# Output gate formed ahead of the norm factor, weight pieces alone on SP's DMA queue, seven expert blocks issued by ScalarE, and another rounding order at the delta products

## The chip, the cores and the metric

The kernel runs on 1 core of one Trainium2 chip, in float32. The metric is the device time of one execution in microseconds. A run of a kernel is given with its span (first to last instruction) and the granted clock of TensorE (PE). The other engines are VectorE (DVE), ScalarE (ACT), GpSimd (POOL) and SyncE (SP), which here only issues DMAs.

## What is computed

Two transformer layers over 256 tokens of width 1024; the second adds 16 meta tokens. The part around the change is the end of the second layer's mixer and its mixture of experts:

```python
o = rms_norm_2(o, out_norm_g) * jax.nn.silu(zf)               # o: sum of the forward and the backward delta rule
y_d = o.reshape(bsz, seq_len, V_WIDTH) @ w_delta
merged = jax.nn.sigmoid(gate_f) * y_f + jax.nn.sigmoid(gate_d) * y_d
h = h + merged @ w_out
hn = rms_norm_2(h, norm_g)                                    # then a router: top group of 8, top 2 of its 8 experts
out = sum over chosen experts e of weight * (silu(hn @ w_gate[e]) * (hn @ w_up[e])) @ w_down[e]
```

There are 64 experts of width 256; gate and up together are 2 MB an expert, down 1 MB: 201 MB that all have to be read.

## The kernel before

**Engines and order.** Every engine has its own program written out by hand, with counting semaphores between them. `fill(name, ...)` gives a PSUM bank to a result, `full[b]` and `free[b]` count its fills and releases, `got(name)` waits for a fill. DMAs start in the order of the issuing engine's program, and an engine that waits holds back everything behind it, its DMA issues too. In this kernel SP issues all loads; ScalarE issues only two of the four stores at the end.

**Products with float32 accuracy from rounded parts.** A weight is cut into a high part (ScalarE, `ACT.Copy` to fp32r) and a low part (POOL, raw minus high), an activation likewise (ScalarE high, DVE low). `matmul3` then makes three products: high x low, high x high, low x high. `w_delta` and `w_out` come as 16 pieces (`N_PARTS`) of 512 KB, eight each, in five buffers (`PART_SETS`); piece n+5 may be loaded when piece n has been used (`part_done`, `load_part`). A piece is 24 products of 128x128 by 256 columns. ScalarE cuts it in `round_part(n)` (L1819), POOL in L2975. The first two pieces of each weight are taken together in `first_two` (L889): it goes through the activation in four pairs of rows and waits for each pair's high part (`h_hi`), then for its low part.

**The norm and the gate of o.** DVE adds up o in `add_out` (L2583) and counts `o_b`. ScalarE squares it (`out_squares`, L1829, into `o_sq`), PE sums the squares (`norms`, fill `no`), ScalarE takes the root (`norm_sqrt`, L1657), DVE the reciprocal and its split (`factors`, L2361 to L2366), and PE spreads the factor over the partitions (`out_spread`, L1220, fills `os00` to `os11`). `out_gated(j)` on DVE (L2699) multiplies a pair of heads in PSUM by o and the gain `out_g` (L2702), and then by silu(z), which lies in `z_g` (L2704). `delta_hi(j)` (L1841) rounds the result, `out_lo(j)` (L2706) makes the low part, and PE starts on `wd0`, the first two pieces. The results `wd0` to `wd3` are gated with `g_g` and added to the Fourier part (L2725, L2726), rounded by `sum_hi(j)` (L1847), and go on to `wp0` to `wp4`, the output product. Then follow the router and the lists of chosen tokens.

**Experts.** 16 groups of 4 experts. A group needs four `gate_up` blocks and two `down` blocks of 2048 KB. Groups 0, 2, ... use `gate_up[0]`, four slots of the weight ring; groups 1, 3, ... `gate_up[1]`. `down` has three buffers, `down_a`, `down_b`, `down_c`. A block of a later group is loaded into a buffer when the group there has been used (`part_used`, `gate_up`, `down`). The eleven blocks that have room at first are issued before group 0 starts. Block j of `gate_up[0]` lies in ring slot (2, 3, 0, 1)[j]; slot 2 held `qd`, slot 3 `z_g` and `g_g`, and slots 0 and 1 hold weight pieces, so blocks 3 and 2 wait for the last two pieces (`part_done(14)`, `part_done(15)`).

**SP's order in this stretch** (L3076 to L3111): pieces 0 and 1; after `o_b` 4 the router's weights and block 0 of group 0; after the last product on block `GD + 1` pieces 2 to 4, two down blocks, pieces 5 to 12, block 2 of group 1, pieces 13 to 15, block 3 of group 1; after the last merged rows block 1 of groups 0 and 1; then blocks 3 and 2 of group 0 and 0 of group 1.

Of the kernel before, what the change touches and what calls it, by code (L numbers as in the profile page):

```python
# [70 lines left out]
def build(nc, A):  # L71
    f32, f32r = mybir.dt.float32, mybir.dt.float32r
    ALU, ACT, AX = mybir.AluOpType, mybir.ActivationFunctionType, mybir.AxisListType
    ctx = ExitStack()
    with ctx:
        sems = {}

        def sem(name):
            if name not in sems:
                sems[name] = ctx.enter_context(nc.semaphore(name))  # L80
            return sems[name]
# [47 lines left out]
        def col(name, j=0):  # L129
            a = COLS[name][0]  # L130
            return cols[:, a + j:a + j + 1]
# [10 lines left out]
        full = [sem(f"bank{b}_full") for b in range(8)]  # L142
        free = [sem(f"bank{b}_free") for b in range(8)]
        fills, uses, turn, readers = {}, [0] * 8, {}, {}
# [16 lines left out]
        WHOLE_SLOT = (0, 1, 0, 1, 2, 3, 0, 1)  # L161
# [15 lines left out]
        N_PARTS, PART_SETS = 16, (0, 1, 4, 2, 3)  # L177
# [66 lines left out]
        o_T, y_delta_lo_r = chunked(both(HEADS * SEQ), HEADS)  # L244
# [166 lines left out]
        down_a, down_b = (place(BLOCK) for _ in range(2))  # L411
# [50 lines left out]
        def two(bank):  # L462
            return bank[:, :].rearrange("p (j t) -> p j t", j=2)
# [972 lines left out]
        def _(act):  # L1436
# [68 lines left out]
            f = got("c")  # L1505
# [146 lines left out]
            def norm_sqrt(name, n, ready, signal, lead=True):  # L1652
                f = fills[name]
                if lead:
                    lead_for(name)
                act.wait_ge(sem(ready[0]), ready[1])
                link(nc.scalar.activation(f.bank[:, 0:n], f.bank[:, 0:n], ACT.Sqrt))  # L1657
                act.sem_inc(sem(signal), 1)
# [56 lines left out]
            def take_gate(kind, j):  # L1715
                f = got(f"{kind}{j}")
                gate, func = {"zz": (z_g, ACT.Silu), "gd": (g_g, ACT.Sigmoid)}[kind]
                link(nc.scalar.activation(gate[:, j], two(f.bank), func))
                act.sem_inc(free[f.b], 1)
                act.sem_inc(sem("z_g"), 1)  # L1720
# [98 lines left out]
            def round_part(n):  # L1819

                arrived, count = part_in(n)
                act.wait_ge(arrived, count)
                nc.scalar.activation(set_hi[part_set(n)], set_raw[part_set(n)], ACT.Copy).then_inc(sem("w_hi"), 1)
# [5 lines left out]
            def out_squares(half):  # L1829
                act.wait_ge(sem("o_b"), 2 * half + 2)  # L1830
                heads = slice(4 * half, 4 * half + 4)
                link(nc.scalar.activation(o_sq[:, heads, :], o_T[:, heads, :], ACT.Square))
                act.sem_inc(sem("o_sq"), 1)

            out_squares(0)
            out_squares(1)
            norm_sqrt("no", SEQ, ("ss_o", 1), "sd_o")
            take_gate("gd", 3)
            round_part(2)

            def delta_hi(j):  # L1841

                act.wait_ge(sem("h_rows"), 8 + j + 1)
                nc.scalar.activation(y_delta_hi_r[:, 2 * j:2 * j + 2, :], two(fills[f"os{j // 2}{j % 2}"].bank),
                                     ACT.Copy).then_inc(sem("h_hi"), 1)

            def sum_hi(j):  # L1847

                act.wait_ge(sem("h_rows"), 12 + j + 1)
                nc.scalar.activation(y_sum_hi_r[:, 2 * j:2 * j + 2, :], two(fills[f"wd{j}"].bank), ACT.Copy).then_inc(sem("h_hi"), 1)  # L1850

            for j in range(4): delta_hi(j)
            round_part(3)
            round_part(4)
            for j in range(4):
                sum_hi(j)
                round_part(2 * j + 5)
                round_part(2 * j + 6)
            round_part(13)
# [97 lines left out]
        def _(dve):  # L1957
            def got(name):
                f = fills[name]
                dve.wait_ge(full[f.b], f.n + 1)  # L1960
                return f
# [3 lines left out]
            def link(ins):  # L1965

                chain[0] += 1
                ins.then_inc(sem("dve_chain"), 1)
                dve.wait_ge(sem("dve_chain"), chain[0])
# [613 lines left out]
            def add_out(l):  # L2583
                f = got(f"o{l.key}")
                o = o_T[:, l.hs[0]:l.hs[0] + 4, l.at - META:l.at - META + P]
                link(nc.vector.tensor_tensor(o, o, four_of(f.bank), ALU.add))
                dve.sem_inc(free[f.b], 1)
                dve.sem_inc(sem("o_b"), 1)
# [106 lines left out]
            for l in (b0, b1, f0, f1): take_values(l)  # L2695
            dve.wait_ge(sem("o_first"), 4)
            for l in (f0, b0, f1, b1): add_out(l)

            def out_gated(j):  # L2699
                f = got(f"os{j // 2}{j % 2}")  # L2700
                o = two(f.bank)
                link(nc.vector.scalar_tensor_tensor(o, o_T[:, 2 * j:2 * j + 2, :], col("out_g"), o, ALU.mult, ALU.mult))  # L2702
                dve.wait_ge(sem("z_g"), j + 1)
                nc.vector.tensor_tensor(o, o, z_g[:, j], ALU.mult).then_inc(sem("h_rows"), 1)  # L2704

            def out_lo(j):  # L2706
# [280 lines left out]
        def _(sp):  # L2987
# [28 lines left out]
            def load_gate_up(q, u, js=range(PER)):  # L3016
                for j in js:
                    name = "odd_in" if u else f"slot{WHOLE_SLOT[4 + j]}_in"
                    sp.dma_start(gate_up[u][j], of_group("gate_up", q, j)).then_inc(sem(name), 16)
                    sp.sem_inc(sem("late_odd" if u else "late_even"), 16 if u else 32)  # L3020
# [14 lines left out]
            def load_down_first(q, u):  # L3035

                sp.dma_start(down[u][0], of_group("down", q, 0)).then_inc(sem("down_c_in" if u else "down_a_in"), 16)

            def load_down_second(q):

                sp.dma_start(down_b, of_group("down", q, 1)).then_inc(sem("down_b_in"), 16)
                sp.sem_inc(sem("late_down"), 16)
# [27 lines left out]
            def load_part(n):  # L3070

                if n >= 5:
                    part_done(n - 5)
                sp.dma_start(set_raw[part_set(n)], FRONT[WD + n // 4][:, n % 4 * QUARTER:(n % 4 + 1) * QUARTER]).then_inc(part_in(n)[0], 16)
# [4 lines left out]
            load_part(1)  # L3079
            sp.wait_ge(sem("o_b"), 4)  # L3080
            sp.dma_start(w_router, A["w_router"]).then_inc(sem("router_in"), 16)
            load_gate_up(0, 0, [0])
            last = readers[f"block{GD + 1}"]
            sp.wait_ge(full[last.b], last.n + 1)
            load_part(2)
            load_part(3)
            load_part(4)
            load_down_first(0, 0)
            load_down_second(0)
            for n in range(5, 13): load_part(n)  # L3090
            load_gate_up(1, 1, [2])
            for n in range(13, N_PARTS): load_part(n)
            load_gate_up(1, 1, [3])
            sp.wait_ge(sem("merged2"), 4)
            load_gate_up(0, 0, [1])
            load_gate_up(1, 1, [1])
            part_done(14)
            load_gate_up(0, 0, [3])
            part_done(15)
# [150 lines left out]
```

## Time and profile before

| | |
|---|---|
| median of 3 runs | 1168.56 us (1168.13 to 1171.38) |
| the profiled execution | 1165.79 us, span 1164.0 us, mean clock 0.938 |
| busy | PE 1015.5 us (87%), PEld 799.3, DVE 508.6, ACT 380.5, POOL 427.6 |
| matmuls | 8121 |
| read from HBM | 302.67 MB |
| chain that ended last | PE 51%, DMA 26%, DVE 14% |

The profiled execution is one run. Its times are microseconds from the start of the span. "SPq" and "ACTq" are the sequencers' own instructions, DMA issues among them; a bracket at the end of a timeline row gives the idle time before it and what ended that. In the chain each piece is work that the end waited for. The clock is given as a share of the full 2.4 GHz. Matmuls overlap, so the duration of a single one is longer than its step in the chain.

### The profile page before, as it was taken

To read this page: it belongs to the slowest core of one execution; us is meant where nothing else is said; L and a number is where in the kernel's file an instruction comes from. 1 tells how busy PE (TensorE), PEld (TensorE's weight loads), DVE (VectorE), ACT (ScalarE), POOL (GpSimd) and SP (SyncE) were. 2 spreads that over 40 slices of the span, in tenths; PEclk is the share of its full clock that TensorE was granted. 3 is DMA by queue.
4 is the path that set the end of the run, shared out by engine and by line. 5 is a ranking of instruction groups with operands and counts; after the bars stand their busy time and mean duration, and the time that the engine had idled before them with its cause. 6 is when DMAs were issued, how large, how long until landed. Compare 5 with 4: busy or idle time off the path is not lost.

```text
span 1164.0 us, 20100 instructions
## 1 busy us (share of the span) xinstructions
PE 1015.5 (87%) x8121; PEld 799.3 (69%) x8121; DVE 508.6 (44%) x979; ACT 380.5 (33%) x572; POOL 427.6 (37%) x192
## 2 busy tenths in 40 slices
PE   9999999999999998899989899977667676676687
PEld 7999999999999998798989798433223232333232
DVE  4356965601136887768864634222222222222213
ACT  5554353444447556335343344100000000000002
POOL 5767868888876856333031271000000000000000
PEclk8999999999999999999999899988888888888889
DMA  7645546566656545115211789999999999999995
GB/s 247 212 134 151 178 128 183 179 183 186 188 172 212 150 124 162 56 54 218 81 66 37 311 284 409 379 426 428 427 428 427 428 428 428 429 427 429 426 424 230
DMA packets 43569, 304.75 MB, mean 262 GB/s; under 512 B 5092, under 2 KB 5476, under 8 KB 30952
## 3 DMA queue, kind: packets, MB, share of 16 engines
q1 hardware_dynamic: 43208, 303.21, 69.2%
q8 instruction: 51, 0.84, 0.3%
q10 hardware_dynamic: 288, 0.52, 0.1%
q14 instruction: 22, 0.18, 0.1%
HBM read 302.67 MB, written 1.05 MB: 261 GB/s over the span
## 4 chain that ended last, share of the span: by engine, by line
PE 51%; DMA 26%; DVE 14%; issue 3%; POOL 2%; ACT 2%; SPq 2%; DVEq 0%; ACTq 0%; POOLq 0%
DMA arena<-gate_up 24%; PE bank L486 10%; PE bank L487 9%; PE bank L488 9%; PE bank L1363 7%; PE bank L871 3%; PE bank L1384 3%; DVE arena L2352 2%; POOL rounded L2975 1%; DMA weights<-front 1%; DVE arena L2099 1%; POOL rounded L2934 1%; DVE arena L2551 1%; DVE arena L2549 1%; DMA arena<-down 1%
## 5 line engine op out<-in xcount | busy, mean ns | idle before, releaser
L2934 POOL TENSOR_TENSOR rounded<-weights,rounded 128x1024 fp32r<-128x1024 f32 x152 | 370.4, 2464 | 160.3 <-ACT rounded L1449 150.5
L486 PE MATMUL bank<-rounded 128*128 128x256 f32 (+2 forms) x776 | 219.7, 283 | 2.3 <-POOL rounded L2934 2.3
L487 PE MATMUL bank<-rounded 128*128 128x256 f32 (+2 forms) x776 | 217.1, 280 | 0.0
L488 PE MATMUL bank<-rounded 128*128 128x256 f32 (+2 forms) x776 | 216.7, 279 | 0.0
L1449 ACT ACTIVATE rounded<-weights 128x1024 fp32r<-128x1024 f32 x146 | 147.4, 1052 | 81.0 <-PE bank L488 49.4
L486 PE MATMUL bank<-rounded,rounded 128*128 128x256 f32 (+3 forms) x552 | 159.1, 288 | 3.7 <-DVEq L2354 1.6
L487 PE MATMUL bank<-rounded,rounded 128*128 128x256 f32 (+3 forms) x552 | 156.7, 284 | 0.0
L488 PE MATMUL bank<-rounded,rounded 128*128 128x256 f32 (+3 forms) x552 | 156.5, 284 | 0.0
L486 PEld LDWEIGHTS bank<-rounded 128*128 128x128 f32 (+1 forms) x776 | 145.7, 188 | 4.4 <-POOL rounded L2934 3.0
L487 PEld LDWEIGHTS bank<-rounded 128*128 128x128 f32 (+1 forms) x776 | 145.7, 188 | 0.7 <-issue 0.7
L488 PEld LDWEIGHTS bank<-rounded 128*128 128x128 f32 (+1 forms) x776 | 145.4, 187 | 0.0
L1363 PE MATMUL bank<-arena 128*32 128x512 f32 x512 | 73.6, 738 | 50.7 <-DMA arena<-gate_up 50.7
L1363 PE MATMUL bank<-weights,arena 128*32 128x512 f32 x512 | 69.3, 702 | 49.2 <-DMA weights<-gate_up 48.1
L486 PEld LDWEIGHTS bank<-rounded,rounded 128*128 128x128 f32 (+1 forms) x552 | 103.8, 188 | 6.7 <-issue 1.9
L487 PEld LDWEIGHTS bank<-rounded,rounded 128*128 128x128 f32 (+1 forms) x552 | 103.8, 188 | 0.2
L488 PEld LDWEIGHTS bank<-rounded,rounded 128*128 128x128 f32 (+1 forms) x552 | 103.7, 188 | 0.1
L2842 DVE TENSOR_TENSOR arena<-arena,bank 128x256 f32<-128x256 f32 x16 | 6.8, 422 | 211.6 <-ACT arena L1908 211.6
L1363 PEld LDWEIGHTS bank<-arena 128*32 128x32 f32 x512 | 17.8, 131 | 100.9 <-DMA arena<-gate_up 52.4
L1363 PEld LDWEIGHTS bank<-weights,arena 128*32 128x32 f32 x512 | 17.8, 127 | 95.2 <-issue 95.2
L1908 ACT ACTIVATE arena<-bank 128x256 f32<-128x256 f32 x16 | 6.1, 384 | 230.4 <-PE bank L1363 230.4
L1396 PE MATMUL bank<-arena 128*128 128x512 f32 x128 | 59.3, 605 | 12.6 <-DVE arena L2847 12.6
L1327 PEld LDWEIGHTS bank<-arena 128*128 128x128 f32 x512 | 59.5, 192 | 8.3 <-issue 8.3
(467 smaller groups left out, 1445.1 us busy)
## 6 DMA issues: line engine op xcount, KB each, us to landing
weights<-front SPq DMA_DIRECT2D x165, 512.0 KB, 4.2
arena<-down SPq DMA_DIRECT2D x31, 2048.0 KB, 21.6
weights<-gate_up SPq DMA_DIRECT2D x28, 2048.0 KB, 34.3
arena<-gate_up SPq DMA_DIRECT2D x28, 2048.0 KB, 33.3
weights<-front SPq DMA_DIRECT2D x4, 2048.0 KB, 8.1
weights<-gate_up SPq DMA_DIRECT2D x8, 768.0 KB, 13.2
arena<-gate_up SPq DMA_DIRECT2D x4, 1536.0 KB, 33.3
weights<-gate_up SPq DMA_DIRECT2D x4, 512.0 KB, 6.2
```

The costliest lines, as they stand in the source:

```text
L486: nc.tensor.matmul(out, a[0], b[1], start=start, stop=False)
L487: nc.tensor.matmul(out, a[0], b[0], start=False, stop=False)
L488: return nc.tensor.matmul(out, a[1], b[0], start=False, stop=stop)
L871: last = nc.tensor.matmul(f.bank[:, j * n:(j + 1) * n], w[:, c:c + P], x[:, k, :], start=k == 0, stop=k == KD - 1)
L1327: last = nc.tensor.matmul(o, m_tok[:, t, k * P:(k + 1) * P], pick_m[:, t, :], start=t == 0, stop=t == TT - 1)
L1363: last = nc.tensor.matmul(banks[3][j * CAP:(j + 1) * CAP, :], xg[:, k, j * CAP:(j + 1) * CAP], gate_up[u][j][:, k * 2 * FE:(k + 1) * 2 * F ...
L1384: last = nc.tensor.matmul(banks[5 + half][j * CAP:(j + 1) * CAP, :], hid_T[:, i, j * CAP:(j + 1) * CAP], down[u][j // 2][:, c:c + 512], st ...
L1396: nc.tensor.matmul(banks[b][:, :], pick_T[:, i % 2 * P:(i % 2 + 1) * P], yb[:, i // 2 * 512:(i // 2 + 1) * 512], start=True, stop=True).th ...
L1449: nc.scalar.activation(w_hi[h % SPLIT][:, quarter(q)], raw[q % RAW], ACT.Copy).then_inc(sem("w_hi"), 1)
L2099: link(nc.vector.scalar_tensor_tensor(s, r[:, h, :], wi[:, t * NH + h:t * NH + h + 1], causal if h == 0 else s, ALU.mult, ALU.add))
L2352: link(nc.vector.scalar_tensor_tensor(dst[:, lo:hi], x[:, first + lo + s:first + hi + s], tap(j), dst[:, lo:hi], ALU.mult, ALU.add))
L2934: nc.gpsimd.tensor_tensor(lo, raw[q % RAW], hi.bitcast(f32), ALU.subtract).then_inc(sem("w_lo"), 1)
```

## The change

Four edits. DVE multiplies `z_g` in place by o and `out_g`, four heads at a time, right after `add_out`; `out_gated` then only multiplies the spread factor by it. On ScalarE `round_part(2)` moves from ahead of the four `delta_hi` to behind them. SP no longer loads seven expert blocks: ScalarE issues block 0 of group 0 and the first down block behind `out_squares(1)`, the second down block and blocks 2 and 3 of group 1 behind `norm_sqrt`, and block 1 of groups 0 and 1 behind `sum_hi(3)`. On SP piece 2 is loaded once the sum of squares (`no`) is there, pieces 3 to 15 from the end of block `GD + 1` on, with nothing between them, and the wait for the merged rows is gone.

```diff
--- before.py
+++ after.py
@@ -1832,11 +1832,26 @@
                 link(nc.scalar.activation(o_sq[:, heads, :], o_T[:, heads, :], ACT.Square))
                 act.sem_inc(sem("o_sq"), 1)
 
+            def load_even(j):
+
+                act.dma_start(gate_up[0][j], A["gate_up"][0, j]).then_inc(sem(f"slot{WHOLE_SLOT[4 + j]}_in"), 16)
+                act.sem_inc(sem("late_even"), 32)
+
+            def load_odd(j):
+
+                act.dma_start(gate_up[1][j], A["gate_up"][1, j]).then_inc(sem("odd_in"), 16)
+                act.sem_inc(sem("late_odd"), 16)
+
             out_squares(0)
             out_squares(1)
+            load_even(0)
+            act.dma_start(down_a, A["down"][0, 0]).then_inc(sem("down_a_in"), 16)
             norm_sqrt("no", SEQ, ("ss_o", 1), "sd_o")
+            act.dma_start(down_b, A["down"][0, 1]).then_inc(sem("down_b_in"), 16)
+            act.sem_inc(sem("late_down"), 16)
+            load_odd(2)
+            load_odd(3)
             take_gate("gd", 3)
-            round_part(2)
 
             def delta_hi(j):
 
@@ -1850,10 +1865,14 @@
                 nc.scalar.activation(y_sum_hi_r[:, 2 * j:2 * j + 2, :], two(fills[f"wd{j}"].bank), ACT.Copy).then_inc(sem("h_hi"), 1)
 
             for j in range(4): delta_hi(j)
+            round_part(2)
             round_part(3)
             round_part(4)
             for j in range(4):
                 sum_hi(j)
+                if j == 3:
+                    load_even(1)
+                    load_odd(1)
                 round_part(2 * j + 5)
                 round_part(2 * j + 6)
             round_part(13)
@@ -2695,12 +2714,13 @@
             for l in (b0, b1, f0, f1): take_values(l)
             dve.wait_ge(sem("o_first"), 4)
             for l in (f0, b0, f1, b1): add_out(l)
+            dve.wait_ge(sem("z_g"), 4)
+            for half in range(2):
+                z = z_g[:, 2 * half:2 * half + 2].rearrange("p j k t -> p (j k) t")
+                link(nc.vector.scalar_tensor_tensor(z, o_T[:, 4 * half:4 * half + 4, :], col("out_g"), z, ALU.mult, ALU.mult))
 
             def out_gated(j):
-                f = got(f"os{j // 2}{j % 2}")
-                o = two(f.bank)
-                link(nc.vector.scalar_tensor_tensor(o, o_T[:, 2 * j:2 * j + 2, :], col("out_g"), o, ALU.mult, ALU.mult))
-                dve.wait_ge(sem("z_g"), j + 1)
+                o = two(got(f"os{j // 2}{j % 2}").bank)
                 nc.vector.tensor_tensor(o, o, z_g[:, j], ALU.mult).then_inc(sem("h_rows"), 1)
 
             def out_lo(j):
@@ -3079,21 +3099,11 @@
             load_part(1)
             sp.wait_ge(sem("o_b"), 4)
             sp.dma_start(w_router, A["w_router"]).then_inc(sem("router_in"), 16)
-            load_gate_up(0, 0, [0])
+            sp.wait_ge(full[fills["no"].b], fills["no"].n + 1)
+            load_part(2)
             last = readers[f"block{GD + 1}"]
             sp.wait_ge(full[last.b], last.n + 1)
-            load_part(2)
-            load_part(3)
-            load_part(4)
-            load_down_first(0, 0)
-            load_down_second(0)
-            for n in range(5, 13): load_part(n)
-            load_gate_up(1, 1, [2])
-            for n in range(13, N_PARTS): load_part(n)
-            load_gate_up(1, 1, [3])
-            sp.wait_ge(sem("merged2"), 4)
-            load_gate_up(0, 0, [1])
-            load_gate_up(1, 1, [1])
+            for n in range(3, N_PARTS): load_part(n)
             part_done(14)
             load_gate_up(0, 0, [3])
             part_done(15)
```

## Rows read from the trace of the kernel before

**Rows 1.** Busy time by stage, core 0: PE, PEld, DVE, ACT, POOL, clock, DMA share, GB/s
```profile
652.00:726.00 74.00, 66.59 (x534) 64.05 (x534) 37.28 (x86) 32.54 (x50) 34.08 (x18) 0.95 0.91 359
726.00:730.00 4.00, 3.86 (x36) 1.24 (x40) 0.29 (x1) 0.00 (x0) 0.00 (x0) 1.00 0.40 119
730.00:1150.00 420.00, 308.36 (x2152) 133.09 (x2144) 87.84 (x179) 31.92 (x65) 0.00 (x0) 0.87 1.00 424
```

**Rows 2.** The chain that ended last, in time: start us, us, what
```profile
651.67 4.02 DMA arena<-front
...
656.77 0.50 ACT rounded L1844
...
664.88 5.26 DMA weights<-front
670.16 1.07 ACT rounded L1823
...
683.41 0.36 PE bank L898
...
686.48 1.41 PE bank L906 x12
...
726.14 7.07 PE bank L1363 x64
```

**Rows 3.** The timeline of SP, its DMA issues: start us, us, what
```profile
644.81 0.43 SPq L3019 DMA_DIRECT2D weights<-gate_up  x1
...
652.99 0.43 SPq L3037 DMA_DIRECT2D arena<-down  x1
...
728.12 6.94 SPq L3027 DMA_DIRECT2D weights<-gate_up  x12
```

**Rows 4.** The timeline of ScalarE, ahead of the delta products
```profile
644.45 1.06 ACT L1832 ACTIVATE arena<-arena 128x1024 f32<-128x1024 f32 x1 [2.52 <-DVEq L2588]
645.61 1.28 ACT L1657 ACT_TABLE_LOAD   x1
648.58 0.37 ACT L1657 ACTIVATE bank<-bank 128x256 f32<-128x256 f32 x1 [1.69 <-DVEq L2362]
...
651.68 0.60 ACT L1718 ACTIVATE weights<-bank 128x512 f32<-128x512 f32 x1 [1.34 <-PE bank L871]
```

**Rows 5.** The timeline of DVE, same stretch
```profile
643.57 0.69 DVE L2586 TENSOR_TENSOR arena<-arena,bank 128x512 f32<-128x512 f32 x1 [1.10 <-PE bank L1102]
648.06 0.43 DVE L2361 TENSOR_SCALAR bank<-bank 128x256 f32<-128x256 f32 x1 [3.80 <-PE bank L830]
...
652.52 0.76 DVE L2702 SCALAR_TENSOR_TENSOR bank<-arena,bank 128x512 f32<-128x512 f32 x1 [0.75 <-PE bank L1220]
653.31 0.70 DVE L2704 TENSOR_TENSOR bank<-bank,weights 128x512 f32<-128x512 f32 x1
...
658.08 0.68 DVE L2710 TENSOR_TENSOR rounded<-bank,rounded 128x512 fp32r<-128x512 f32 x1
659.00 0.69 DVE L2710 TENSOR_TENSOR rounded<-bank,rounded 128x512 fp32r<-128x512 f32 x1 [0.24 <-ACT rounded L1844]
```

**Rows 6.** Groups of instructions by form, DVE: busy us, mean ns | idle before
```profile
L2924 DVE SCALAR_TENSOR_TENSOR arena<-arena 128x512 f32<-128x512 f32 x2 | 1.4, 750 | 0.0
```

**Rows 7.** The waits of PE from 600 to 730: total us, times, longest
```profile
PE bank L898 <- ACT rounded L1844: 4.2, 1, 4.2
```

**Rows 8.** Busy time in stretches of 2 us, columns as in rows 1
```profile
656.00:658.00 2.00, 0.60 (x3) 0.63 (x4) 1.93 (x4) 2.00 (x4) 1.16 (x1) 0.50 1.10 453
...
660.00:662.00 2.00, 2.00 (x13) 2.00 (x12) 1.52 (x3) 0.69 (x1) 2.00 (x1) 0.59 0.97 410
```

**Rows 9.** The timeline of POOL (GpSimd), low parts of the weight pieces
```profile
678.39 7.13 POOL L2975 TENSOR_TENSOR rounded<-weights,rounded 128x1024 fp32r<-128x1024 f32 x3
```

**Rows 10.** The page's DMA queues: packets, MB, share of 16 engines
```profile
q1 hardware_dynamic: 43208, 303.21, 69.2%
...
q10 hardware_dynamic: 288, 0.52, 0.1%
```

## The prediction

> **What bounds the kernel now.** I read the busy time by stage first [rows 1]. From 730 to 1150 us the DMA engines are fully busy at 424 GB/s: the expert weights stream, and PE waits for them. From 652 to 726 us, the delta and output products, PE is busy 66.6 of 74 us while the DMAs carry 359 GB/s. Between them, 726 to 730, the DMAs fall to 119 GB/s: every expert block for which there is room has landed, and the next may be issued only once group 0's products have begun. The first such issue is at 728.12 [rows 3], and from there the stream never stops. The end is therefore the start of group 0's products, 726.14 in the chain [rows 2], plus a fixed length. Filling buffers earlier gives nothing by itself; what counts is how soon 726.14 comes.
>
> Second, the chain through the stage before it [rows 2]. It enters through a weight piece (issued 651.67, landed 4.02 us later, at 655.7), which ScalarE then rounds, the rounding of the first delta rows at 656.77, and PE's first product just after 657.2. PE waited 4.2 us there [rows 7], and its granted clock was 0.50 of full from 656 to 658 [rows 8]. DVE had its first rows ready at 654.0 [rows 5]; ScalarE stood at the piece, ahead of them in its order. Third, the issues of SP [rows 3]: two down blocks follow pieces 3 and 4 at 652.99, and pieces 5 and 6, issued at 664.88, land only at 670.16 [rows 2], 5.3 us instead of 4.0.
>
> **The gate on DVE.** Four multiplies of 0.76 us [rows 5], one ahead of each `z` multiply of 0.70, leave the path after the factor's broadcast. Two of 1024 columns come instead, after the last addition (643.57 + 0.69). The nearest row, 512 columns from SBUF, is 0.75 us [rows 6]; each is then at most 1.5, with 0.24 for the chained wait (659.00 - 658.08 - 0.68 [rows 5]) 3.5 together, so DVE is free at 647.8, and needed at 648.06 [rows 5]. They cost nothing; were they 0.3 us longer, the difference would count once. They wait for the gates of `z`, which are long there. The first rows come at 652.52 + 0.70 = 653.2 and the last at about 655.3.
>
> **The order on ScalarE.** `round_part(2)` goes behind the four roundings of the delta rows. ScalarE finishes the last output gate at 651.68 + 0.60 = 652.3 [rows 4], so it takes the first rows at 653.3, gives them 0.5 us [rows 2], and PE starts at about 654.0 instead of 657.4: 3.4 us. PE's idle stretch shrinks from 4.2 to under 1 us, so I expect no fall of its clock. A product costs 1.41 / 12 = 0.118 us at full clock [rows 2]; at half clock twice that. The clock was half from 656 and 0.59 on the mean of 660 to 662 [rows 8], so about to 661.6: 4.2 us of products that take 2.1. With 48 products of 0.118 the first pair ends at 659.7, where it ended at 664.88 (the issue released by it): 5.2 us. The low parts on DVE, four at steps of 0.92 us [rows 5] from 655.3, end at 659.0 and just keep ahead. What is late next is the split of the pieces. On POOL one takes 7.13 / 3 = 2.38 us [rows 9] against 24 x 0.118 = 2.8 us of PE, so POOL keeps up if the pieces arrive. Piece 9's low part, both wanted at once for pieces 8 and 9, then comes at about 677.8, and PE starts on them at 677.9; before it did so at 683.41 [rows 2]. So far the gain is 5.5 us, and nothing behind it changes: 1168.6 - 5.5 = 1163.1.
>
> **The loads.** The price is here. ScalarE now issues group 0's first block and the first down block behind its second square (644.45 + 1.06, so at 645.7 and 646.1), ahead of a table load of 1.28 us that has to be through by 648.58 [rows 4]: 645.7 + 0.9 + 1.28 = 647.9, so it is. Three more issues follow at 649.0 to 650.3; the next table load ends at about 651.6, and the gate could start at 651.68. The issues themselves cost ScalarE 0.1 us at most. The two behind `sum_hi(3)` hold `round_part(11)` by 0.9 us, with POOL two pieces behind it: nothing. SP loses seven issues and the wait for the merged rows.
>
> But 5 blocks of 2048 KB, 10.5 MB, are now under way from about 647.0. At 424 GB/s a block takes 4.95 us and a piece 1.24 us. The five alone fill the DMA engines until 671.7, and pieces 2 to 6 fall in just that time. Before, one block and two down blocks stood there, all in SP's order, and pieces 2 to 4 went ahead of the down blocks. The rows show one loaded queue and, at the very end, 0.52 MB on ScalarE's [rows 10]; no row shows how a piece fares beside a block on another queue. Its bounds: pieces served first (nothing lost), and pieces served in order of issue or last.
>
> I take turns: one transfer, or one row of it, from either queue. A row of a block is 16 KB and one of a piece 4 KB, so pieces get a fifth of the bytes. With 1.3 us from issue to data and 1.5 from data to landing (1.24 + 2.8 is the 4.0 of piece 2 before [rows 2]; the halves are my guess): the first block until 652.0, piece 2 until 653.2, a block, piece 3 until 659.4, a block, piece 4 until 665.6, a block, piece 5 until 671.8, a block, piece 6 at 677.9 and landed at 679.4. Rounding takes 1.07 [rows 2], POOL 2.38 a piece, so the low parts follow at 682.9, 685.3, 687.7 and, of piece 9, 690.0. PE begins on 8 and 9 at 690.1 instead of 683.4: +6.7 us, gains of the first two edits already in. PE's waits of some 3 us between pieces may also drop its clock, and the two blocks at `sum_hi(3)` may hold piece 13 by up to 1.9 us. I take +7.5: 1168.6 + 7.5 = 1176.
>
> The Trainium skill, "DMA: Bandwidth & Descriptors", section "Queues, rings and completion order", says that each DMA engine goes round the queues that have work and changes only at packet borders. That is the sharing of the forecast; by equal bytes the sum would be 1163. No row here shows it.
>
> **The rivals.** (a) Equal bytes, or pieces first. A piece then takes 2.5 us of a shared stream, faster than PE's 2.8; piece 2 lands before 656, piece 3 at about 657, piece 5 at about 664.4, and the gain of 5.5 us stands: 1163. For it speaks only that SP's pieces were never seen to starve [rows 2], on a queue where nothing could overtake them. This is the end on the other side; it decides where pieces get more than 1.24 / 2.8 = 44% of the bytes. (b) Order of issue across queues. Piece 2 stands behind two blocks, piece 3 behind all five (647.0 + 24.8 + 1.24 + 1.24 = 674.2, landed 675.7). PE takes up piece 3 at 679.3, and 8 and 9 at 693.6: +10.2, 1179. (c) Turns as in the forecast, but each change of queue stops the engine for a while; up to 40 changes lie there, and if each cost 0.5 us, which no row bounds, that is +20 and more: 1190 or above. (d) A share between a fifth and 44%, or loads whose start is later than I have them: within 3 us of now, 1167 to 1171. That the change does not do what it says (ScalarE's issues wait for something) would leave the pieces free, and falls under (a).
>
> **How the numbers follow.** The profiled execution took 1165.79 us with a span of 1164.0; the median of the runs is 1168.56. The shifts are taken from the profiled one and added to the median, since the stream behind them is the same. Chances: forecast (turns) 0.42, (b) 0.14, (c) 0.07, (a) 0.28, (d) 0.09. A measurement of this kernel tells 0.3%, 3.5 us, from no change. Faster is (a), 0.28; same is (d) with a little of the forecast, 0.10; slower the rest, 0.62. The range reaches from (a) with 1 us to spare, 1162, to (b) with the 1.9 us of piece 13 and 3 us of clock, 1184; (c) stays out. The likeliest case by itself spans 1174 to 1180.
>
> **What would show it.** First edit: two DVE multiplies of 1024 columns at 644.5 to 647.8, and one multiply a pair behind the broadcast. Second: PE's first delta product at about 654, no wait of 4.2 us, clock 1.00 at 656 to 662. Loads: a second loaded queue of 14.7 MB in the DMA table, full DMA from 647 on. The forecast wants landing times of pieces 3 to 6 of 8 us and more, ScalarE waiting for them at `round_part`, POOL waiting on ScalarE, PE waiting on POOL some 3 us at each of pieces 3 to 5, and group 0 starting near 733. If those landings stay at 4 to 5 us and group 0 starts at 720 to 721, rival (a) holds and the forecast is wrong. If group 0 starts early and the end does not move with it, my reading of the fixed stream is wrong.

## The result, and the profile after

The changed kernel takes 1184.08 us (median of 4 runs, 1182.12 to 1185.04), the one before 1168.35 us: a ratio of 1.0139, 95% interval 1.0118 to 1.0160. It is slower by 16.2 us by that ratio (15.7 between the medians), where 7.5 were forecast. The profiled execution took 1182.12 us, with a span of 1180.0 us.

I read it in the order of the prediction. First the busy time by stage, columns as in [rows 1]:

```profile
652.00:742.00 90.00, 73.18 (x540) 69.29 (x538) 30.85 (x85) 34.97 (x51) 33.83 (x18) 0.91 0.77 307
742.00:746.00 4.00, 3.68 (x36) 1.24 (x40) 0.47 (x2) 0.00 (x0) 0.00 (x0) 1.00 0.23 65
746.00:1166.00 420.00, 305.34 (x2152) 132.67 (x2144) 87.86 (x179) 31.91 (x65) 0.00 (x0) 0.87 1.00 424
```

The stream of expert weights has the same 424 GB/s and begins 16 us later. The stage of the delta and output products is longer by that: PE idles 17 us of 90 where it idled 7.4 of 74. That the stream is a fixed length shows in SP's issues. The first one after the gap [rows 3] is now

```profile
744.30 6.94 SPq L3047 DMA_DIRECT2D weights<-gate_up  x12
```

and from it to the end of the span there are 1180.0 - 744.30 = 435.7 us, against 1164.0 - 728.12 = 435.9 before. In eleven of the twelve profiles here it is 435.7 to 436.2 us, in e6 437.2.

The two profiled executions already differ ahead of any edit. ScalarE's last output gate but one, which is the same instruction in both, is a good mark (before, then after; the timeline of ScalarE):

```profile
636.42 0.60 ACT L1718 ACTIVATE weights<-bank 128x512 f32<-128x512 f32 x1 [10.48 <-PE bank L871]
```
```profile
638.03 0.60 ACT L1718 ACTIVATE weights<-bank 128x512 f32<-128x512 f32 x1 [10.48 <-PE bank L871]
```

So 1.6 us of the difference lie ahead of it. Among all kernels below the mark stands anywhere from 634.35 to 639.09, with nothing changed before it. So I count every stage from this mark. From it to the first issue of the stream there are 14.6 us more (106.27 instead of 91.70). The 15.7 to 16.2 us of the timed runs are a little more; 14.6 lies within their interval (0.0118 to 0.0160 of 1168, so 13.8 to 18.7 us).

Where they went, in the chain that ended last (start us, us, what), against [rows 2]:

```profile
654.94 0.60 ACT rounded L1859
655.68 0.35 PE bank L898
...
661.17 18.46 DMA weights<-front
679.65 1.07 ACT rounded L1823
...
693.59 0.36 PE bank L898
...
699.08 11.22 DMA weights<-front
710.32 1.06 ACT rounded L1823
711.38 0.53 ACT arena L1889
711.95 1.87 PE bank L1263 x8
```

Two weight pieces stand in it, piece 5 and piece 13, with 18.5 and 11.2 us from issue to landing; before, it held piece 2 with 4.0 and piece 5 with 5.3. ScalarE's timeline has all pieces of the stretch: a bracket is its wait for the landing.

```profile
647.22 0.40 ACTq L1837 DMA_DIRECT2D weights<-gate_up  x1
647.72 0.37 ACTq L1848 DMA_DIRECT2D arena<-down  x1
...
650.74 0.33 ACTq L1850 DMA_DIRECT2D arena<-down  x1
651.18 1.05 ACTq L1842 DMA_DIRECT2D arena<-gate_up  x2
...
654.94 2.39 ACT L1859 ACTIVATE rounded<-bank 128x512 fp32r<-128x512 f32 x4 [0.72 <-DVE bank L2724]
660.68 1.06 ACT L1823 ACTIVATE rounded<-arena 128x1024 fp32r<-128x1024 f32 x1 [3.35 <-DMA arena<-front]
667.30 1.06 ACT L1823 ACTIVATE rounded<-weights 128x1024 fp32r<-128x1024 f32 x1 [5.57 <-DMA weights<-front]
673.47 1.06 ACT L1823 ACTIVATE rounded<-weights 128x1024 fp32r<-128x1024 f32 x1 [5.10 <-DMA weights<-front]
...
679.65 1.06 ACT L1823 ACTIVATE rounded<-weights 128x1024 fp32r<-128x1024 f32 x1 [4.64 <-DMA weights<-front]
```

Pieces 2 to 5 land at 660.7, 667.3, 673.5 and 679.6 (ScalarE waited for each and rounds it at once), 6.2 to 6.6 us apart, beside five blocks. The waits of PE from 645 to 695 us and from 695 to 745:

```profile
PE bank L486 <- POOL rounded L2995: 10.2, 4, 3.4
PE bank L898 <- ACT rounded L1859: 0.8, 1, 0.8
```
```profile
PE bank L1263 <- ACT arena L1889: 3.5, 1, 3.5
```

The 4.2 us of [rows 7] have become 0.8, and 10.2 and 3.5 us of waiting for pieces have come. The second names a square of the residual; it waits on ScalarE behind the rounding of piece 13, so it too is a wait for a piece. In before ScalarE took up piece 13, issued at 689.10, after 5.0 us:

```profile
694.09 1.06 ACT L1823 ACTIVATE rounded<-weights 128x1024 fp32r<-128x1024 f32 x1 [6.45 <-DMA weights<-front]
```

### The profile page after: what moved, and what is told of

The parts are those of the page before. It is cut to its first block, busy times and chain, and to the rows that moved or that the text cites. A ratio compares the mean times of both kernels' runs of the same rounds, so it can differ in the third digit from the quotient of the medians.

```text
span 1180.0 us, 20095 instructions
## 1 busy us (share of the span) xinstructions
PE 1018.6 (86%) x8121; PEld 804.0 (68%) x8121; DVE 502.1 (43%) x977; ACT 381.1 (32%) x572; POOL 426.4 (36%) x192
## 3 DMA queue, kind: packets, MB, share of 16 engines
HBM read 302.67 MB, written 1.05 MB: 257 GB/s over the span
## 4 chain that ended last, share of the span: by engine, by line
PE 51%; DMA 28%; DVE 13%; issue 3%; ACT 2%; SPq 2%; POOL 1%; DVEq 0%; ACTq 0%; POOLq 0%
DMA arena<-gate_up 24%; PE bank L486 10%; PE bank L488 10%; PE bank L487 10%; PE bank L1363 6%; DMA weights<-front 3%; PE bank L1384 3%; PE bank L871 2%; DVE arena L2371 2%; DMA arena<-down 1%; DVE arena L2118 1%; DVE arena L2570 1%; DVE arena L2568 1%; SPq L3039 1%; PE bank L1102 1%
## 5 line engine op out<-in xcount | busy, mean ns | idle before, releaser
L486 PE MATMUL bank<-rounded,rounded 128*128 128x256 f32 (+3 forms) x552 | 162.4, 294 | 13.5 <-POOL rounded L2995 10.2
L487 PE MATMUL bank<-rounded,rounded 128*128 128x256 f32 (+3 forms) x552 | 159.3, 289 | 0.0
L488 PE MATMUL bank<-rounded,rounded 128*128 128x256 f32 (+3 forms) x552 | 159.2, 288 | 0.0
L486 PEld LDWEIGHTS bank<-rounded,rounded 128*128 128x128 f32 (+1 forms) x552 | 106.7, 193 | 17.2 <-POOL rounded L2995 6.8
L1363 PE MATMUL bank<-arena 128*32 128x512 f32 x512 | 69.7, 704 | 51.3 <-DMA arena<-gate_up 51.3
L488 PEld LDWEIGHTS bank<-rounded,rounded 128*128 128x128 f32 (+1 forms) x552 | 106.7, 193 | 0.1
L487 PEld LDWEIGHTS bank<-rounded,rounded 128*128 128x128 f32 (+1 forms) x552 | 106.6, 193 | 0.1
## 6 DMA issues: line engine op xcount, KB each, us to landing
weights<-gate_up SPq DMA_DIRECT2D x8, 768.0 KB, 13.1
```

Source lines behind the costliest of these rows:

```text
L486: nc.tensor.matmul(out, a[0], b[1], start=start, stop=False)
L487: nc.tensor.matmul(out, a[0], b[0], start=False, stop=False)
L488: return nc.tensor.matmul(out, a[1], b[0], start=False, stop=stop)
L1363: last = nc.tensor.matmul(banks[3][j * CAP:(j + 1) * CAP, :], xg[:, k, j * CAP:(j + 1) * CAP], gate_up[u][j][:, k * 2 * FE:(k + 1) * 2 * F ...
```

## Experiments

The table has, for each kernel's profiled run, the time from the mark to PE's first product on pieces 8 and 9 (A, 46.99 us before), from there to SP's first issue of the stream (B, 44.71 before), and the ratio to before of the timed runs. After stands first.

| kernel | A, against before | B, against before | both | ratio, 95% interval |
|---|---|---|---|---|
| after | 55.56, +8.6 | 50.71, +6.0 | +14.6 | 1.0139 (1.0118 to 1.0160) |
| e1 | 47.59, +0.6 | 44.29, -0.4 | +0.2 | 0.9988 (0.9970 to 1.0007) |
| e2 | 56.03, +9.0 | 50.27, +5.6 | +14.6 | 1.0138 (1.0114 to 1.0163) |
| e3 | 58.24, +11.3 | 47.41, +2.7 | +14.0 | 1.0143 (1.0118 to 1.0167) |
| e4 | 60.08, +13.1 | 52.38, +7.7 | +20.8 | 1.0170 (1.0144 to 1.0196) |
| e5 | 52.97, +6.0 | 46.38, +1.7 | +7.7 | 1.0055 (1.0032 to 1.0078) |
| e6 | 55.50, +8.5 | 44.30, -0.4 | +8.1 | 1.0096 (1.0072 to 1.0120) |
| e7 | 48.42, +1.4 | 53.68, +9.0 | +10.4 | 1.0089 (1.0060 to 1.0117) |
| e8 | 43.88, -3.1 | 44.71, 0.0 | -3.1 | 0.9978 (0.9965 to 0.9992) |
| e9 | 43.99, -3.0 | 44.70, 0.0 | -3.0 | 0.9981 (0.9961 to 1.0001) |
| e10 | 47.45, +0.5 | 46.21, +1.5 | +2.0 | 1.0011 (0.9995 to 1.0028) |

A and B come from one profile each, the ratios from several runs with intervals of 1.5 to 3.3 us to either side. Where they differ most (e6: +8.1 and 11.2 us) the profile shows one run, the fastest of its four. In it the stretch behind B is 1.3 us longer than before's, and nothing shows where the others lost the rest.

### e1 and e2: the two halves of the change

e1 is before with the gate's and the rounding's edits alone; e2 is before with the load edit alone. Both are parts of the diff above, nothing else.

> The kernel before with the gate on z_g and the later place of round_part(2), all loads on SP as before. Theory: these two edits gain and the loads alone lose. DVE has its first rows 0.8 us earlier, ScalarE takes them at once, PE starts on the delta products 3.4 us earlier and at full clock: 5 us less, ratio about 0.9957 (0.994 to 0.997), and PE's wait of 4.2 us is gone. Rival: the early start is given back at the first piece that comes late (pieces 5 and 6 still stand behind two down blocks on SP's queue and can't land before about 668): then under 2.5 us, ratio 0.998 or more, with PE waiting on POOL at piece 5. Rival that the edits themselves cost (DVE's two long multiplies hold the norm factor): ratio 1.000 or above.

> The kernel before with only the loads changed as in the kernel after: seven blocks on ScalarE's queue, pieces alone on SP's; gate and rounding order as before. Theory: pieces and blocks take turns row by row, a piece lands every 6.1 us while blocks are under way, and this sets PE's pace from piece 3 on, so the late start of the first pair (round_part(2) waits for piece 2 until about 660) is hidden: as long as the kernel after within 2 us, ratio 1.012 to 1.016. Rival: costs add up, the loads cost 21 us by themselves and the other edits gave 5 back: ratio 1.018.

e1: 1166.56 us, 0.9988, no difference that can be told: the theory's 0.994 to 0.997 was missed, and its first rival is what came. The edits did on PE what they were to do (its first delta product waits 0.8 us), and it was given back. PE's waits of e1 in the stretch, and the piece in its chain:

```profile
PE bank L486 <- POOL rounded L2976: 5.4, 1, 5.4
...
PE bank L898 <- ACT rounded L1843: 0.8, 1, 0.8
```
```profile
659.56 10.33 DMA weights<-front
669.92 1.06 ACT rounded L1823
```

Pieces 5 and 6 are now issued at 659.56 instead of 664.88, but land at 669.9 instead of 670.1: the two down blocks, issued at 652.8 and 653.3, are ahead of them in SP's queue. PE now waits 5.4 us for piece 5, and that is the 5.3 us by which it was early.

e2: 1183.95 us, the same as after. PE's waits in e2:

```profile
PE bank L898 <- ACT rounded L1860: 7.1, 1, 7.1
PE bank L486 <- POOL rounded L2994: 5.4, 2, 3.7
```

Without the edits the first product waits 7.1 us for piece 2; with them the same time is waited a little later. So the whole loss is the loads', and in the full change the other two edits are hidden.

### e3 and e5: the size of a row

e3 is after with each of ScalarE's blocks issued as two DMAs with rows of 4 KB, e5 as two halves with rows of 8 KB (shortened; in both PE also waits for all second halves ahead of group 0):

```diff
-                act.dma_start(gate_up[0][j], A["gate_up"][0, j]).then_inc(...)
+                half = lambda x, i: x[:, i * HALF:(i + 1) * HALF]          # e5: half a row, 8 KB
+                for i in range(2):
+                    act.dma_start(half(dst, i), half(src, i)).then_inc(...)
```

> The kernel after, each of the seven blocks issued by ScalarE as two DMAs with rows of 4 KB (quarters 0 and 2, quarters 1 and 3 of a partition's 16 KB) instead of one with rows of 16 KB. Same bytes, same queue, same places, seven issues more on ScalarE (0.4 us each, of which under 1 us lies ahead of the first delta rows). Theory of turns by row: a piece now gets half of the bytes, 8 x 2 x 0.159 = 2.5 us instead of 6.1, faster than PE's 2.8: the stall goes, and the kernel ends near 1164 to 1167, ratio to before 0.996 to 0.999. Rival, bytes ahead of the pieces count, not rows (the queues are served in order of issue, or by whole transfers): nothing changes, ratio 1.012 to 1.018.

> The kernel after, with each of ScalarE's blocks issued as two DMAs of 1024 KB, whose rows are 8 KB instead of 16 KB; the computation is the same. One change of size only, which should leave ScalarE free to issue (90 rows a DMA engine for the five blocks, where the 4 KB rows stopped it). Theory (turns row by row): pieces get a third of the bytes, so one comes every 3.8 us instead of 6.2 between pieces 2 and 6; pieces 3 to 6 are no longer what PE waits for by more than 1 us at a time, delta_hi is at 655 as in after, and the products on pieces 8 and 9 start some 5 us sooner than in after. The end moves with it only as far as piece 13 lets it: ratio to before 1.006 to 1.011. Rival (only the bytes ahead of a piece count, or the ends are tied to the last of the bytes, not to the pieces): 1.012 to 1.018, as after.

e3's total did not move (1.0143), and it can't be read as it was meant. ScalarE's timeline:

```profile
652.82 12.04 ACTq L1840 DMA_DIRECT2D arena<-gate_up  x4
664.97 1.28 ACT L1719 ACT_TABLE_LOAD   x1 [13.79 <-issue]
```

ScalarE stood 12.04 us in four DMA issues, where the two in after took 1.05 us together. Its rounding of the delta rows came at 667.1 and PE waited 12.4 us. That the queue was full is my inference; no row shows its depth. What can be read in e3 is that pieces 2 to 4 arrived 2.6 and 3.2 us apart (by the ends of their rows in the DMA packet records) instead of 6.2, and that its B is 3.3 us shorter than after's.

e5 issues the same four DMAs in 1.95 us, and the end moved: 1174.27 us, 1.0055, 9.8 us less than after, a little more than I had expected. A is only 2.6 us shorter (5 were expected). Pieces 2 and 3 are 3.7 us apart as forecast, but the next steps are 5.1, 6.7 and 4.2 us (again by the ends of their rows). For the first of these no row gives a cause. The second is a late issue: PE's first product had to wait 1.7 us for ScalarE, its clock was 0.65 from 652 to 660 us, and so it freed the slots of pieces 5 and 6 only 27.7 us behind the mark (663.70), in after 23.1 (661.17). B is 4.3 us shorter. The bytes, their order of issue and the queues are the same; the rows and the DMAs are half as long. The rival, that only the bytes ahead count, falls. Turns by whole DMA instead of by row would also give 3.7 us in e5 (half a block, 4.95 / 2, and a piece, 1.24), so the step alone doesn't tell the two apart. The packet records do.

These records don't name the engine; I put one engine's together from records whose end is the next one's start. One of the 16 in after (the records' clock is 11.1 us ahead of the page's; queue, bytes, start us, ns):

```
ScalarE  16384  659.510  2049      SP       4096  665.389   159
ScalarE  16384  661.556   614      ScalarE 16384  665.544   611
ScalarE  16384  662.166   618      SP       4096  666.156   159
ScalarE  16384  662.781   618      ScalarE 16384  666.311   611
ScalarE  16384  663.395   620      SP       4096  666.918   159
ScalarE  16384  664.011   611      ScalarE 16384  667.073   611
ScalarE  16384  664.618   615      SP       4096  667.681   159
SP        4096  665.230   159      ScalarE 16384  667.836   611
```

From 665.389 on it is one row from either queue in turn, with no gap between them; later two rows of one queue follow each other at single places, as at 665.230 here. A turn costs 611 + 159 = 770 ns, and a piece, 8 rows on each engine, 6.16 us. In e5 the records alternate 309 and 159 ns. But seven rows of ScalarE's go first (six to eight on the other engines). The first block was issued 2.44 us ahead of piece 2 (647.22 and 649.66), and its first row began 5.72 us ahead of piece 2's (659.51 and 665.23): the piece lost 3.3 us before its first turn. In e5 mostly 13 rows of 8 KB stand there, again 4.0 us. It is not the start of a DMA as such: in e6, where no block stands beside piece 13, that piece's first row begins 0.95 us after its issue, in after 3.63. Nor is it a fixed number of rows. My reading, that these rows had been fetched by the engine already, was not tested.

The Trainium skill, "DMA: Bandwidth & Descriptors", section "Queues, rings and completion order", has each engine go round the queues and take a whole packet of typically 9 to 17 descriptors from one before it changes. That it goes round agrees. A turn here is one row, 611 ns for one queue and 159 ns for the other; of how many descriptors a row is made no record shows. If a row is one descriptor, the page's count is too high here, and the measurement decides.

### e4: the same blocks from SP

e4 is after with the seven blocks issued by SP at the same places of its order, so that all stands in one queue.

> The kernel after, with the seven blocks issued by SP, at the same places: one block and a down block ahead of piece 2, the second down block and two blocks of group 1 behind piece 2, the last two when the merged rows are done, behind piece 12. One queue, served in order. Theory: the queue as such doesn't matter, the bytes that get ahead of a piece do. Piece 3 then stands behind all five blocks and lands at about 676 to 678, later pieces follow at 1.2 us each; PE starts on pieces 8 and 9 about 10 us later than before: ratio 1.009 to 1.014. Rival: it is ScalarE's issuing, or having two queues at all, that costs: ratio 1.003 or less.

1188.01 us, 1.0170, 3.9 us above after (the intervals overlap) and above the 1.009 to 1.014 of the theory, which had A some 10 us longer and nothing for piece 13; measured are +13.1 and, in B, +7.7. PE's waits, and the taking up of piece 3:

```profile
PE bank L486 <- POOL rounded L2986: 16.4, 3, 12.8
PE bank L1263 <- ACT arena L1880: 4.2, 1, 4.2
```
```profile
676.57 1.06 ACT L1823 ACTIVATE rounded<-weights 128x1024 fp32r<-128x1024 f32 x1 [14.96 <-DMA weights<-front]
```

A is 4.5 us longer than after's. This is what rival (b), the order of issue, looks like: one wait of 12.8 us at piece 3 instead of four of up to 3.4. Counted from the mark, piece 3 is there at 675.7 of before's time, the figure of (b), and in after at 665.7. So ScalarE's queue is not what costs. The blocks ahead of the pieces are, and by A the second queue even softens it; the timed runs don't tell e4 from after for certain.

### e6 and e7: the second pair of blocks

e6 is after with blocks 1 of groups 0 and 1 back on SP, behind piece 15. e7 is e1 with this pair alone on ScalarE, and so without SP's wait for the merged rows:

```diff
             for j in range(4):
                 sum_hi(j)
-                if j == 3:          # after; taken away in e6, added to e1 in e7
-                    load_even(1)
-                    load_odd(1)
```

> The kernel after, with the second pair of blocks (block 1 of group 0 and of group 1) issued by SP behind piece 15 and the merged rows, as in before, instead of by ScalarE at sum_hi(3); the first five blocks stay on ScalarE. Theory: piece 13 then has no block beside it and lands 4 us after its issue instead of 11.2, PE's wait at it (10.2 us in 3 places, this one 3.5 to 4) goes, and group 0 starts 4 to 6 us sooner than in after: ratio to before 1.008 to 1.011. Rival (piece 13 is late because its slot comes free late, not because of the blocks): 1.012 to 1.016, the same as after. A second way for it to stay: the pair now lands later than group 0 wants it.

> The kernel before with the gate and rounding edits (as e1_gate_order), and of the load edit only the second pair: block 1 of group 0 and of group 1 issued by ScalarE at sum_hi(3). Theory: this part alone costs the wait at the pieces that follow the pair, 4 to 6 us against e1_gate_order: ratio to before 1.0025 to 1.005. If that cost needs the late pieces before it, it is nothing: 0.997 to 1.001.

They split the loss. e6, 1178.40 us, 1.0096: A stays as in after (+8.5), and B is that of before. There is no PE wait behind 695 us that before had not. After owes 6.4 us of B to the pair. e7, 1176.68 us, 1.0089: A stays near e1's, B grows by 9.4 us over e1's. The pair costs it by itself, more than I had expected (4 to 6 us). In e7 SP's own block 2 of group 1 (issued 685.26) stands ahead of piece 13 as well; that this is the reason was not tested. The piece was issued at 690.65, and ScalarE took it up 13 us later:

```profile
703.71 1.06 ACT L1823 ACTIVATE rounded<-weights 128x1024 fp32r<-128x1024 f32 x1 [13.58 <-DMA weights<-front]
```

The time lost is more than the wait. In after PE waits 3.5 us at this place, and B is 6.0 longer; in e7 5.1 and 9.4. Three stretches of after, the wait and what follows it, show the rest (columns as in [rows 1]):

```profile
708.00:712.00 4.00, 0.49 (x5) 0.35 (x4) 0.00 (x0) 1.57 (x2) 0.55 (x1) 0.85 0.77 312
712.00:716.00 4.00, 3.96 (x18) 3.88 (x19) 0.00 (x0) 2.43 (x3) 3.28 (x2) 0.50 0.05 22
716.00:720.00 4.00, 4.00 (x31) 4.00 (x30) 1.07 (x3) 0.65 (x2) 3.23 (x2) 0.79 0.02 4
```

After 3.5 us without work the granted clock is 0.50 (the 1.2 GHz level) and then 0.79, and 49 products start from 712 to 720 where 74 do in such a time at 1.00 (before, 692 to 700). In e7 it is 0.50 from 704 to 712 us. The last column tells a second thing: with the pair landed the DMA engines carry 22 and 4 GB/s here, where e1 carried 422 and 426 in the same two stretches.

### e8, e9 and e10: the edits with another order of loads

e1 named what was missing: pieces 5 and 6 ahead of the down blocks. All three keep every load on SP. The three edits in one, shortened:

```diff
             load_gate_up(0, 0, [0])
+            sp.wait_ge(full[fills["no"].b], fills["no"].n + 1)
+            load_part(2)
+            load_down_first(0, 0)                      # e8; e9, e10: behind piece 4
             last = readers[f"block{GD + 1}"]
             sp.wait_ge(full[last.b], last.n + 1)
-            load_part(2)
             load_part(3)
             load_part(4)
-            load_down_first(0, 0)
+            for n in range(5, 7): load_part(n)         # e9, e10: 5 to 8
             load_down_second(0)
-            for n in range(5, 13): load_part(n)
+            for n in range(7, 13): load_part(n)        # e9, e10: 9 to 12
```

e8 and e9 have the gate's and rounding's edits, e10 is e9 without them.

> A candidate to beat both: the gate and rounding edits, every load on SP, in another order: piece 2 and the first down block right behind the norm's sums (ahead of the wait for the last product on block GD + 1), then pieces 3 to 6, then the second down block, then pieces 7 to 12 and on as before. Theory: e1_gate_order gave its gain back at pieces 5 and 6, which stood behind two down blocks; here they come ahead of one of them and behind the other by 5 us, so they are in time, PE keeps its earlier start, and group 0 starts 4 to 5.5 us sooner: ratio to before 0.995 to 0.997. Rival (the stage is bound by the bytes it has to carry, so a gain at one piece turns up as a wait at a later one): 0.998 to 1.001.

> The gate and rounding edits with every load on SP, in a further order: piece 2 behind the norm's sums, then after the last product on block GD + 1 pieces 3 and 4, the first down block, pieces 5 to 8, the second down block, pieces 9 to 12, and on as before. Theory, from e8_pieces_between: there piece 3 landed behind a down block, so that POOL began its run at 664.5 instead of 661.7, and piece 7 landed 8.9 us after its issue behind the other. With each block one or two pieces later POOL runs through, the products on pieces 8 and 9 start 1 to 2.4 us sooner than in e8_pieces_between, and the ratio to before is 0.9955 to 0.997. Rival (the gain is at its end, or the down blocks are now late for group 0): 0.9975 to 1.000.

> The kernel before with the load order of e9_downs_later alone, without the gate and rounding edits. Theory: with an early piece 2 ScalarE's rounding of the delta rows no longer waits for a piece, so that part of PE's 4.2 us goes even without the edits (rows at 654.0, so PE starts at 656 to 656.5 instead of 657.4), and the rest of the gain needs them: ratio to before 0.998 to 1.000, 1.5 to 3.5 us above e9_downs_later. Rival (the order of the loads alone gives it all, and the gate and rounding edits nothing): the same as e9_downs_later within 1 us.

e8: 1165.85 us, 0.9978, interval 0.9965 to 0.9992. It is faster than before by 2.6 us (2.1 between the medians), the only kernel here whose interval lies below 1, though its upper bound is hardly below; 0.995 to 0.997 had been expected. e9: 0.9981 with A as in e8, so the further step gave nothing, where 1 to 2.4 us had been expected. PE's waits in e9:

```profile
PE bank L486 <- POOL rounded L2976: 2.1, 1, 2.1
PE bank L898 <- POOL rounded L2976: 1.3, 1, 1.3
```

e8 has 1.6 and 1.4 at the same two places. In e9 POOL had pieces 2 to 4 done at 661.8 and stood until 665.9, for piece 5. That one was issued when the first pair freed its slot, at 657.69, behind the first down block.

e10: 1.0011 (0.998 to 1.000 expected), 3.5 us above e9 by the ratios, and 5.0 in A and B. So neither the order alone (+1.3 us) nor the edits alone (-1.4 us) can be told from nothing. Together they give 2.2 us in e9, whose interval just reaches across 1, and 2.6 in e8's order. In A and B it is +2.0, +0.2 and -3.0. PE's waits in e10:

```profile
PE bank L898 <- POOL rounded L2975: 3.9, 1, 3.9
PE bank L898 <- ACT rounded L1844: 2.7, 1, 2.7
```

The second is the 4.2 us of before, shortened by the early piece 2. The first is piece 9, now behind the second down block.

## Why the forecast was right in kind and wrong in size

Times of after are given less 1.6 us here, to stand beside the forecast's.

**The fixed stream** was right (435.7 and 435.9 us).

**The gate on DVE and the order on ScalarE** were right to tenths. DVE's two multiplies (its timeline):

```profile
646.47 2.60 DVE L2720 SCALAR_TENSOR_TENSOR weights<-arena,weights 128x1024 f32<-128x1024 f32 x2 [0.60 <-DVE arena L2605]
```

That is 1.30 each, under the bound of 1.5. PE's first delta product came at 654.1 (654.0 forecast), and the first pair ended at 659.6 (659.7). What failed is the sentence behind it, "nothing behind it changes: 1168.6 - 5.5". I had looked at POOL's pace and assumed that pieces 5 and 6 would arrive as much earlier as they were issued. With the old order of loads they don't, and the gain is lost (e1); [rows 3] had the two down blocks just ahead of them. With the pieces ahead of a down block 3.0 to 3.1 us remain in A and B (e8, e9). In after this step cost nothing more, since the late pieces hide both edits (e2). My estimate from e8 and e9 is that even rival (a), where the down blocks leave SP's queue, would have ended nearer to 1166 (1168.6 - 3.0) than to 1163; no run shows it.

**Turns** were right. The period was forecast at 6.2 us and measured at 6.6, 6.2, 6.2; the raw records show one row each, and so a fifth of the bytes for the pieces. (b) was wrong: it has piece 3 at 675.7, where e4 has it, and in after it lands at 665.7. That its 693.6 for pieces 8 and 9 is the figure in the trace of after is chance (without the 1.6 us it is 692.0). (c) was wrong: a change of queue leaves no gap. (d) was wrong: the share is not above a fifth.

**The first pieces**, +6.7 forecast, +8.6 measured. Piece 2 landed at 659.1, not 654.7, and pieces 3 to 5 were 4.7 or 4.8 us later than forecast. I had let piece 2 pass after the first block as one transfer; by rows it needs eight turns, 6.2 us, from its first row, and seven rows of the block go first. Of the 4.4 us, piece 6 kept only 1.1 (landed 680.5, forecast 679.4), since the blocks had run out by then. For the rest of the 1.9 two things stand in the trace, whose parts nothing here separates: PE's clock behind its waits (0.50 from 672 to 676 and 0.63 from 684 to 688, in the trace's own time), and ScalarE's order (piece 9 is rounded at 689.80, behind a rounding of sums that had to wait for DVE).

**Piece 13** is the term that failed: up to 1.9 us forecast with 0.8 put into the sum, 6.0 measured (6.4 against e6). The mechanism was named, the size was wrong for two reasons. By row turns a piece beside two blocks of 16 KB rows takes 6.2 us, and the rows that go first another 4 (its own first row began 3.63 us after its issue on one engine, later on the others). So it landed 11.2 us after its issue, where it took 5.0 before and 3.7 in e6. The prediction gives no working for its 1.9. It did not apply to piece 13 the turns that it applied to pieces 2 to 6. And the stall brings half the clock behind it, which I had kept to the range and out of the sum.

So of the 14.6 us, 8.6 are the five blocks beside pieces 2 to 6, and 6.0 the pair beside piece 13. With 1168.6 + 14.6 = 1183.2 the sum would have been within 1 us of the result. The range ended at 1184 and the result is 1184.08. That it came so near is luck: the upper end was built from rival (b), which is wrong, and held 1.9 us for piece 13, whose landing came 6.2 us later than before's 5.0.

**Left open**: whether the rows that go first had been fetched already, how deep ScalarE's queue is, and why the mark moves by up to 4.7 us from one profiled run to the next.

## What to carry to other kernels

Two queues on the same engines share by rows and not by bytes: work out a small urgent transfer's landing as its rows times (its row + the other queue's row), and some 4 us more before its first turn when its queue was empty, for every such transfer beside the bulk one, and cut the bulk rows or move the bulk behind the urgent ones. An edit that makes an engine ready earlier gains only if the loads that its earlier progress triggers also arrive earlier; look up what stands ahead of them in their queue before writing the gain down. A stall of PE can cost more than its length: behind 3.4 us and more of waiting the products here ran at half clock for a time (behind 1.6 and 2.1 us, in e8 and e9, at full clock), so price them too.

## What the runs showed of the hardware

- Two loaded queues alternate row by row on each DMA engine (611 and 159 ns in after, 309 and 159 ns in e5) without a pause between them. A newly loaded queue had its first turn only after about 4 us of rows of the other one: mostly seven of 16 KB (after) or 13 of 8 KB (e5).
- A DMA issue can hold the engine that issues it. In e3 ScalarE stood 12.04 us in four issues, with 4 KB rows in its blocks; with 8 KB rows the same four took 1.95 us.
- A profile may be shifted as a whole. Ahead of everything edited, the same instruction started from 634.35 to 639.09 us, and 1.6 of the 16.0 us between the spans of before and after was that alone.
